# One attention stage: the prompt's differential heads beside twenty of the sample's differential units

## What is computed

```
def diff_core(q, k, v, qpos, kpos, bias_b, lam, lam_init, subln_g):
    logits = einsum('bqhcd,bkhcd->bhcqk', q, k) * (B_HEAD_DIM ** -0.5)
    logits = logits + bias_b[rel_bucket(qpos[:, None] - kpos[None, :])]
    p = softmax(where(kpos <= qpos, logits, -inf))
    w = p[:, :, 0] - lam * p[:, :, 1]
    o = einsum('bhqk,bkhe->bqhe', w, v)
    o = rmsnorm(o, subln_g) * (1.0 - lam_init)

def indexer_scores(qi, wi, ki):
    dots = einsum('bqhd,bkd->bqhk', qi, ki) * (IDX_DIM ** -0.5)
    return einsum('bqhk,bqh->bqk', relu(dots), wi * (IDX_HEADS ** -0.5))
```

## Time and profile before

| what | us |
|---|---|
| median of 3 runs (lowest to highest) | 2587.86 (2584.32 to 2591.13) |
| the profiled execution, its own time | 2581.11 |
| span of its trace | 2579.3 |
| differential stage, from its first logits | 417.0 to 594.5 |
| selective and sample stage, up to the next stage's first matmul | 594.5 to 1317.4 |

### The profile page before, as it was taken

How to read it: one execution, slowest core, us unless ns; L and a number is a source line. 1 busy time by engine, 2 the same in 40 slices (tenths; PEclk the granted TensorE clock), 3 DMA queues, 4 the chain that set the end, 5 groups by cost and what they waited for, 6 DMA issues and landing times. The chain is left out here.

```text
span 2579.3 us, 32477 instructions
## 1 busy us (share of the span) xinstructions
PE 2339.3 (91%) x12461; PEld 1574.9 (61%) x12461; DVE 1090.7 (42%) x2441; ACT 688.9 (27%) x1721; POOL 679.4 (26%) x722
## 2 busy tenths in 40 slices
PE   6999997885788888888889898989999999999999
PEld 4644444563455555555544445548888888888887
DVE  4479997881245533244323212253433343371001
ACT  2321112453555445544411014311111111110000
POOL 1020121112465455556601010013222121201110
PEclk9999997997999999998999999999999999999999
DMA  3211101004699789865640204111111111122221
GB/s 135 74 60 71 42 1 41 1 1 147 233 340 335 250 311 325 301 191 164 177 168 0 70 12 163 41 60 34 50 34 50 34 51 46 38 65 75 75 61 41
DMA packets 148605, 281.74 MB, mean 109 GB/s; under 512 B 14485, under 2 KB 83780, under 8 KB 148452
## 3 DMA queue, kind: packets, MB, share of 16 engines
q0 software_dynamic: 49408, 176.19, 20.1%
q1 hardware_dynamic: 80756, 90.50, 10.7%
q10 hardware_dynamic: 18288, 12.98, 1.7%
HBM read 261.68 MB, written 17.94 MB: 108 GB/s over the span
## 5 line engine op out<-in xcount | busy, mean ns | idle before, releaser
L607 PE MATMUL PS<-region 128*128 128x512 f32 (+5 forms) x864 | 330.6, 538 | 4.1 <-DMA region<-w_in 4.1
L2575 PE MATMUL PS<-region,ffn_w 128*128 128x264 f32 x1408 | 323.4, 388 | 1.6 <-PEq L2026 1.6
L2575 PEld LDWEIGHTS PS<-region,ffn_w 128*128 128x128 f32 x1408 | 269.4, 191 | 48.6 <-issue 2.0
L607 PEld LDWEIGHTS PS<-region 128*128 128x128 f32 (+1 forms) x864 | 154.3, 183 | 166.5 <-issue 140.6
L2575 PE MATMUL PS<-region,side 128*128 128x264 f32 x1056 | 243.3, 387 | 1.5 <-POOL side L2532 1.5
L1816 ACT COPY region<-PS 128x512 f32<-128x512 f32 x352 | 193.6, 594 | 183.4 <-PE PS L1695 96.5
L2575 PEld LDWEIGHTS PS<-region,side 128*128 128x128 f32 x1056 | 198.9, 190 | 35.0 <-POOL side L2532 1.6
L851 DVE TENSOR_SCALAR_CACHE_REDUCE mask<-score,cand 128x384 bf16<-128x384 f32 (+2 forms) x198 | 181.5, 942 | 3.2
L1559 POOL DMA_INDIRECT region<-cache_b_v,gather_b x128 | 122.6, 958 | 90.1 <-PE PS L1778 53.0
L2530 POOL TENSOR_TENSOR side<-ffn_w 128x512 f32<-128x512 f32 x22 | 29.2, 1326 | 391.7 <-DMA ffn_w<-w_gate 197.6
L1778 PE MATMUL PS<-region,sa_pt 128*32 128x512 f32 (+1 forms) x1024 | 86.4, 470 | 28.1 <-DMA region<-cache_b_v,gather_b 19.9
(11 more groups left out here) (429 smaller groups left out, 3977.3 us busy)
## 6 DMA issues: line engine op xcount, KB each, us to landing
ffn_w<-w_gate SPq DMA_DIRECT2D x11, 1024.0 KB, 5.4
ffn_w<-w_up SPq DMA_DIRECT2D x11, 1024.0 KB, 5.5
region<-w_in SPq DMA_DIRECT2D x4, 2048.0 KB, 7.9
ffn_w<-w_down ACTq DMA_DIRECT2D x7, 704.0 KB, 5.4
region<-x_prompt ACTq DMA_DIRECT2D x8, 512.0 KB, 7.3
region<-x_prompt SPq DMA_DIRECT2D x8, 512.0 KB, 10.6
mem_keys<-cache_mem_k SPq DMA_DIRECT2D x8, 512.0 KB, 4.6
mem_values<-cache_mem_v SPq DMA_DIRECT2D x8, 512.0 KB, 7.6
```

The source lines that it names most:

```text
L607: last = nc.tensor.matmul(M.PS[0:n, s % 3, 0:chunks[j].width], XT[:, c, t * P:t * P + n], w[j % 2][:, c, 0:chunks[j].width], start=(c == 0 ...
L2575: last = nc.tensor.matmul(M.PS[:, bank, 0:TW], left[:, c, :], right[:, c, :], start=begin and c == 0, stop=(c == KH - 1), skip_group_check ...
```

## The change

There is one attention stage now, in two halves, and 20 of the 32 B units run in its first half (`Walk.EARLY`).

- First half: the sample's B units 0 to 19 (and one chunk of new tokens) beside the prompt's differential heads. Their steps are L (logits, bias, maxima), E (exponentials, combination), T, V, and once a block N (norm: DVE, then POOL's power), R (scaling, DVE, in SBUF) and M (turning). The heads have one slot pair, one `prob`, one `pt` and one output bank: the combination overwrites `prob`, the transposes overwrite the logits' slot, and the logits of head n wait for the squares of head n-1 (`o_sq`). No count steps c are in this half. Key buffers are single here: `aside` and its two further buffers are used after unit 20 only, since they lie where `KTB` and the values of the prompt lie.
- Second half: the indexer, B units 20 to 31, A units, beside the selective pairs. Three c steps for each chunk instead of two.
- `beside` gets costs: L and E count 3.0 and other prompt steps 1.0, so that most sample steps stand behind L and behind E; an i step counts 4.0. First half: 145 sample and 152 prompt steps, of which 128 are L, E, T, V. Second half: 254 and 128.
- The relus of the indexer go from ACT (one instruction for a step) to DVE (two).
- POOL follows the same merged order; the last key step of unit 19 and its outputs release the first indexer gathers.
- The barrier between the two stages is gone. The clearing of semaphores stands ahead of the joint stage. `bias_a` lies in `KTB` now, so its load waits until the last differential logits (`s_ready`), and the first selective pair waits for all squares, all turned blocks and the end of the prompt's search (`freed`). Several small tiles moved to other places; their sizes aren't changed.

```diff
+    steps = []
+    for n, (i, h) in enumerate(heads):
+        begun = h == 0 and i > 0
+        steps += [("L", n)] + [("R", i - 1)] * begun + [("E", n)] + [("M", i - 1)] * begun + [("T", n), ("V", n)]
+        if h == B_H - 1:
+            steps.append(("N", i))
+    steps += [("R", NB - 1), ("M", NB - 1)]
...
+    prob = M.X[:, 0:2, :]
+    pt = M.X[:, 2, :].rearrange("p (k q) -> p k q", q=P)
+    mix = M.X[:, 3, :].rearrange("p (e n) -> p e n", e=2)
...
+    def sync(eng):
+        eng.dma_start(M.bias_b, head_bias(M, A_H, 12)).then_inc(b_loaded, 16)
+        rows = io["p_b_v"][0, 0].rearrange("(t p) h d -> p t (h d)", p=P)
+        for x, (a, b) in enumerate(((0, 2), (2, NB))):
+            eng.dma_start(M.VB[:, a:b, :], rows[:, a:b, :]).then_inc(v_loaded[x], 16)
+        eng.wait_ge(s_ready, 2 * N)
...
+    def pe(eng):
+        for what, n in steps:
+            if what == "L":
+                i, h = heads[n]
+                nk = (i + 1) * P
+                if n:
+                    eng.wait_ge(o_sq, n)
+                if turned_blocks(n):
+                    eng.wait_ge(m_read, turned_blocks(n))
+                for a, b in parts(0, nk):
...
+            elif what == "T":
+                eng.wait_ge(comb_done, n + 1)
+                for blocks in groups(n):
+                    for kb in blocks:
+                        last = nc.tensor.transpose(slot(0, kb * P, (kb + 1) * P), prob[:, 0, kb * P:(kb + 1) * P],
+                                                   K("ident"))
+                    last.then_inc(tr_done, 1)
+            elif what == "V":
+                i, h = heads[n]
+                if h == 0 and i in (0, 2):
+                    eng.wait_ge(v_loaded[i // 2], 16)
+                for x, blocks in enumerate(groups(n)):
+                    eng.wait_ge(pt_ready, groups_before(n) + x + 1)
+                    for kb in blocks:
+                        last = nc.tensor.matmul(M.PS[:, 2, 0:P], pt[:, kb, :], M.VB[:, kb, h * P:(h + 1) * P],
+                                                start=(kb == 0), stop=(kb == i))
+                last.then_inc(pv_done, 1)
...
+            elif what == "M":
+                eng.wait_ge(mix_done, n + 1)
+                if n < NB - 1:
+                    eng.wait_ge(s_used, 2 * (B_H * (n + 1) + 1))
+                for h in range(B_H):
+                    last = nc.tensor.transpose(M.PS[:, 3, h * P:(h + 1) * P], mix[:, n % 2, h * P:(h + 1) * P], K("ident"))
+                last.then_inc(mt_done, 1)
...
+    def act(eng):
+        for what, n in steps:
+            if what == "E":
+                nk = (heads[n][0] + 1) * P
+                for k in range(2):
+                    eng.wait_ge(max_done, 2 * n + k + 1)
+                    nc.scalar.activation(prob[:, k, 0:nk], slot(k, 0, nk), ACT.Exp, bias=negmax[:, k:k + 1],
+                                         accum_out=psum_[:, k:k + 1]).then_inc(s_used, 1)
+            elif what == "T":
+                for x, blocks in enumerate(groups(n)):
+                    a, m = blocks[0], len(blocks)
+                    eng.wait_ge(tr_done, groups_before(n) + x + 1)
+                    nc.scalar.copy(pt[:, a:a + m, :], slot(0, a * P, (a + m) * P).rearrange("p (k q) -> p k q", k=m)
+                                   ).then_inc(pt_ready, 1)
+            elif what == "V":
+                i, h = heads[n]
+                eng.wait_ge(pv_done, n + 1)
+                nc.scalar.copy(mix[:, i % 2, h * P:(h + 1) * P], M.PS[:, 2, 0:P])
+                nc.scalar.activation(osq[:], M.PS[:, 2, 0:P], ACT.Square, accum_out=oss[:, i % 2, h:h + 1]
+                                     ).then_inc(o_sq, 1)
...
+            elif what == "V":
+                M.top.rounds(link, share)
+            elif what == "N":
+                eng.wait_ge(o_sq, B_H * (n + 1))
+                nc.vector.scalar_tensor_tensor(oms[:, n % 2, :], oss[:, n % 2, :], 1.0 / (2 * HD), eps[:, n % 2, :],
+                                               ALU.mult, ALU.add).then_inc(o_ms, 1)
+            elif what == "R":
+                eng.wait_ge(o_rstd, n + 1)
+                for h in range(B_H):
+                    m = mix[:, n % 2, h * P:(h + 1) * P]
+                    last = nc.vector.scalar_tensor_tensor(m, m, ors[:, n % 2, h:h + 1], M.gain_sub[:], ALU.mult, ALU.mult)
+                last.then_inc(mix_done, 1)
+            elif n == NB - 1 and what == "M":
                 M.top.rounds(link, 1e6)
+                nc.vector.memset(M.sa_score[:, SEGW:SEGW + NS], NEG).then_inc(top_done, 1)
...
+        turn = [step[0] for step in walk.steps].index("i")
+        order = [1, 1] + beside(walk.steps[:turn], b_steps[2:], lambda step: 1.0, lambda step: 3.0 if step[0] in "LE" else 1.0)
+        order += beside(walk.steps[turn:], a_steps, lambda step: 4.0 if step[0] == "i" else 1.0,
+                        lambda step: 3.0 if step[0] in "LE" else 1.0)
...
-                pool_part(pool)
+                run(s_pool(pool), itertools.chain(b_pool(pool), iter(a_steps)))
...
+        self.steps = [("k", 0, j) for j in range(4)] + [("s", 0)]
+        for n in range(end + 1):
+            keys = [("k", n + 1, j) for j in range(1 if self.new(n + 1) else 4)] if n < end else []
+            if n == self.pause:
+                self.steps += [("p", n), ("o", n)]
+                for h in range(NCI):
+                    self.steps += [("i", h, g, a) for g in range(2) for a in range(2)] + [("I", h)]
+                self.steps += keys
+            else:
+                cut = iter(range(33)) if n == 0 else cut
+                late = n > self.pause
+                self.steps += keys[:3] + [("p", n)] + [("c", r) for r in itertools.islice(cut, late)]
+                self.steps += keys[3:] + [("o", n)] + [("c", r) for r in itertools.islice(cut, late)]
+            if n < end:
+                self.steps.append(("s", n + 1))
+                self.steps += [("c", r) for r in itertools.islice(cut, n > self.pause)]
+            if self.new(n):
+                self.steps.append(("f", n))
...
-        return u < self.first_a and u % 2 == 1
+        return self.EARLY < u < self.first_a and (u - self.EARLY) % 2 == 1
...
+        if u in (0, self.EARLY, self.EARLY + 1):
+            return None
+        if u < self.EARLY:
+            return u - 1
...
+        for step in steps:
+            if step[0] == "k" and not walk.new(step[1]):
+                n, j = step[1:]
+                u = walk.unit(n)
+                eng.wait_ge(t_full, fill["k", n, j, 1 if chunks[n][0] == "B" else 0] + 1)
+                if n == walk.pause:
+                    index(0, 0, j)
+                for v in range(len(walk.units)):
+                    if walk.keys_before(v) == u:
+                        keys(v, j)
...
-                relu(rel[:, g, :].rearrange("p (q a e) -> p e a q", a=RKI // 2, e=2)[:, :, 4 * a4:4 * a4 + 4, :],
-                     M.PS[:, L0:L1 + 1, :].rearrange("p e (a q) -> p e a q", a=4), n_i)
...
+        n_i = 0
         for step in steps:
-            if step[0] == "I" and step[1] == NCI - 1:
+            if step[0] == "i":
+                h, g, a4 = step[1:]
+                eng.wait_ge(i_done, n_i + 1)
+                for e in range(2):
+                    last = nc.vector.tensor_scalar(
+                        rel[:, g, :].rearrange("p (q a e) -> p e a q", a=RKI // 2, e=2)[:, e, 4 * a4:4 * a4 + 4, :],
+                        M.PS[:, L0 + e, :].rearrange("p (a q) -> p a q", a=4), HD ** -0.5 * IDX_H ** -0.5, 0.0,
+                        ALU.mult, ALU.max)
+                last.then_inc(relu_done, 1)
```

441 lines of the change are left out of this document (168 added, 273 removed).

## The result

The changed kernel takes 2597.29 us (median of six, 2589.13 to 2598.17) beside 2585.94 for the kernel before (six, 2582.23 to 2591.13). Ratio 1.0042, 95% interval 1.0026 to 1.0057: slower by some 11 us. The forecast was 2573, faster. The time lies inside the range of 2525 to 2615, on the side that had a chance of 0.25.

The account below looks back on a forecast made before the run. PE in its written order was taken as the bound. First half 385 plus second half 500 (56 + 189 + 255) gave 885 against 900 us, so the median 2587.9 less 15: 2573 us, range 2525 to 2615.

Parts of the forecast that it names:

- 385 + 500: The joint stage as first half plus second half: 885 us against 900 before, 15 us less.
- the rest is PE work at some share: Second half after the index part: 383 us of PE work, priced by busy shares of 88.5% and 83.5%.
- Index part 56: Start of second half: eight index steps 34, two score steps 8, four pairs of heads 14, together 56 us.
- The relus hidden: Indexer relus on DVE: 0.7 us per 512 columns, 1.4 a step, hidden beside the next key transposes.
- Twelve units 189: Second half's remaining B units: 167 us of PE work at an 88.5% share, 189 us.
- Last part 255: Sixteen A units and selective pairs: 216 us of PE work at 83.5%, less 4 for the clock, 255 us.
- First half 385: Differential heads beside 20 units: heads 371 us, start 8, block turns 6; PE busy 302 us, 78%.
- The walked chain: One differential head at the last block as a single dependent chain from logits to squares: 13.3 us.
- B: Rival: uncovered head chain; decides from a 12.1 us mean a head, at 13.1 33 us more, 2621; chance 0.18.
- C: Rival: second half takes what the first gives, stretch 906 or 896 us, 2584 to 2594 us; chance 0.17.
- A: Rival: laid-over regimes let PE reach 87% in all parts, 55 us less, 2533 us; chance 0.20.
- The search behind V: First half: the prompt's top-k search on DVE is covered; without cover its 25 counts would be 30 us.

Follow-up runs that it names:

- f1: Changed kernel with all step costs 1.0 in the second half only, first half unchanged: 2552.0 us, ratio 0.9863 to the kernel before.
- flat order: Step order of the changed kernel when all step costs are 1.0; with it in both halves 2551.03 us, ratio 0.9871.
- m_filled: Changed kernel, all step costs 1.0 in both halves, plus five idle transposes ahead of each differential head's transposes: 2545.69 us, ratio 0.9842.
- h_flat: Changed kernel with all step costs 1.0 in both halves, run on a slower chip: 2664.0 us, ratio 0.9794 to the kernel before.
- h_filled: Same slower chip as h_flat, its kernel plus five idle transposes ahead of each differential head's transposes: 2654.0 us, ratio 0.9739.
- h_flat_no_search: h_flat with the rest of the prompt's top-k search left out: 2659.3 us, ratio 0.9771.
- f3: Changed kernel; in the second half index steps cost 1 while L and E keep 3: 2588.4 us, ratio 1.0010.
- f2: Changed kernel; in the second half index steps keep cost 4 while L and E cost 1: 2579.9 us, ratio 0.9986.
- e1_flat: Changed kernel with all step costs 1.0 in both halves, nothing else changed: 2551.03 us, ratio 0.9871 to the kernel before.

## Why the prediction was wrong

The forecast was a gain of 15 us in the sum of "385 + 500"; the stretch became 5.2 us longer, 905.5 instead of 900.3.

**Where the sign came from.** The step that failed is "the rest is PE work at some share": the second half was priced as busy time over a share taken from the stretches of before (88.5% and 83.5%), and the new costs entered only as a number of pairs moved. That the costs also set the distance between E, T and V wasn't priced. The runs show that the costs of the second half are worth 45 us, 2597 to 2552 (f1): they turn a gain of 1.4% (32 us beside the kernel before of the same chip) into a loss of 0.4% (11 us). Without them the forecast's direction would have been right: 2552 is the lower end of its own range (2552 to 2588). The prediction walked one differential head through the order, but never one selective pair.

The miss of the total was made smaller by luck. The terms 385, 56, 189 and 255 describe the flat order, as their shares come from stretches of it; f1 measures 404, 54, 185 and 223, 866 in all. So the order was left out at 40 us in this stretch, and without it the sum was 19 too high: 32 in the last part, less 19 in the first half.

**"Index part 56."** Measured 71. The prediction's work was right (45 and 5, 50 in all; measured 50.9), so the miss is in how long PE stands: 6 us were left for it, and 20 measured. By steps, with the waits ahead of them, the eight index steps took 39.6 us (34 predicted), the two score steps 16.0 (8), the four pairs 15.5 (14). So more than half of the miss is the score steps (L1656), and not the order's doing: they take 16.8 in f1, and already in the kernel before one alone took 8.3 behind a stand of 2:

```profile
633.50 8.32 PE L1651 MATMUL PS<-side,sa_w_sel 128*32 128x512 f32 x16 [2.04 <-ACT side L1820]
```

With flat costs the part takes 54, since index steps fall to 34.2 and three of the four pairs move out of it. "The relus hidden" was right, their size wasn't: DVE took 1.02 us for 512 columns (sixteen, 15.1 us) and not 0.7, so as much as ACT's 1.89 a step, and above the bound of 0.95. Put back on ACT, nothing changed.

**"Twelve units 189"** at 88.5%: measured 196.3 at 84%; f1 184.6 at 89%. The share was right for an order with two steps on each place. **"Last part 255"**: 236. Its work was overpriced, 216 for a measured 194, and the share was right (82%). The prediction took the 190 us of 1086 to 1318 for the sixteen A units. But in the kernel before their first transposes (L1688) come at 1111.8 only; ahead of them 18.7 us of work, the last B unit's, the group's new tokens' and part of a pair's, lie in that stretch. The A units with ten pairs were:

```profile
1111.70:1317.40 205.70, 170.65 (x1613) 114.33 (x1612) 84.40 (x188) 89.89 (x208) 118.57 (x122) 0.94 0.54 154
```

From there, five more pairs added 23 us, 4.6 each and not 5.5. The 19 us that the last part came out shorter hid the other two.

**"First half 385."** Measured 402, and 398 to 405 in six further runs on these chips. The sum of the waits was right: 385 less 302 of work leaves 83 us, and PE stood for 79. The walked chain came out too (13.3, alone 13.8), in part by luck, as said above. The term that was mis-sized is PE's work, 323 instead of 302. The 302 are the heads' 142 of before, at a clock of 0.91, and 20 x 8.0 for the units, whose 8.0 were read where the clock was 0.98. In the first half, whose clock is 0.91 (0.88 on the slower chip), a unit is dearer: from 16 to 20 units PE's busy time there grew by 36 us, 9.0 a unit, and 142 + 20 x 9.0 is 322. At the better clock of m_filled (0.94) the useful work took about 303. That the filling gives back some 10 of the 17 us speaks for the clock as a cause; but h_flat and h_filled, the only pair on one chip, have intervals that just meet, so this is likely and not shown. By heads: 10.0 us at block 0 and 10.5 at block 1 (8.5 and 9.1 predicted), 15.0 and 17.0 at the last two (14.4 and 15.7).

**The rivals.** B's condition was just reached. It named a mean of 12.1 us, (371 + 16)/32, without the 14 us for the start and the turns; measured is (402 - 14)/32, also 12.1. It isn't why the kernel is slower: with the same first half the flat kernels are 32 us faster than before. C's total, 906, is the measured 905.5, by other terms (first half 385, index 66, twelve units 192, last part 263), so by luck. For A, the Trainium skill ("Perfetto Trace Analysis", Optimization Strategy) says that interleaving regimes may gain; the flat kernel agrees, with PE at 83% (717 of 865 us) and not at 87%.

**Costed at nothing.** The search behind V: right (h_flat_no_search). The load of `bias_a`: right, no wait for it is in the lists. The gathers beside the combinations: right within 5 us, as the first half's 160 gathers took 0.96 (keys) and 0.99 us (values) in the mean against 0.94. The 23 of them that overlap a combination (L1181) took 1.08 in the mean, up to 1.73, the others 0.95. The prediction's "0.55 otherwise" was read too widely, though: most of the other powers ran into the start of a combination, which has two SBUF inputs as well, and still took 0.55; only the one that ran wholly beside such an operation took 1.58. The clearing of semaphores: wrong, since it now lies ahead of the first logits, which come 3.7 us later (the stand for PEq there is 5.1 us and was 2.0).

## What to carry to other kernels

When two streams are merged by costs, the costs are not only a balance of work: they set how many foreign steps stand between an instruction and the one that waits for its result. Walk one unit of each stream through the merged order before taking a share of busy time as its price, and look for places with no or one step behind work that another engine must copy. Cut the stretches that give the prices at the events that the names mean, such as the first transposes of the A units, and not near them: 19 us of this prediction's last part were another part's. A busy time holds the clock of the stretch that it was read in. Where PE has to stand for a few microseconds anyway, idle transposes into a free bank may gain a little through the clock; here it was 6 to 10 us of 2550, at the edge of what the runs can tell.

## What the runs showed of the hardware

Short stands of PE were followed by work at either of the two rates, and neither their length nor the instructions decide it. In the changed kernel's index part transposes took 0.24 us each instead of 0.14 behind a stand of 1.62, where slow work had begun already, and 0.14 behind stands of 1.64 and 1.86. The same sixteen score matmuls stand behind the same wait in f1 and in f3, and took 5.37 and 7.04 us:

```profile
870.07 5.37 PE L1655 MATMUL PS<-side,gain_ak 128*32 128x512 f32 x16 [2.02 <-DVE side L1914]
```

```profile
869.74 7.04 PE L1655 MATMUL PS<-side,gain_ak 128*32 128x512 f32 x16 [2.02 <-DVE side L1914]
```

In f2's index part, with 7.0 us of waits before V, the work was some 13 us longer than in f1 (17 less the 4 of the added pairs).

Two chips take 2721 and 2723 us for the kernel before, three others 2583 to 2587. In the flat kernel the extra is all in this stage: the first logits come at 420.7 there and 420.1 here, what lies behind the stage takes 1263 and 1264 us of the span, and this stage 979 and 865. What differs there is seen in the wait lists: ACT, DVE and POOL have waits whose releaser the profile doesn't find ("remote"). Between 415 and 1440 us they come to 115 us for ACT and 77 for DVE in h_flat, and there are none in before, after, e1_flat, f1 or m_filled. Two of h_flat's lines, 857 to 1399 us:

```profile
ACT QTA L1301 <- remote: 45.6, 10, 7.2
...
DVE sa_cmax L1937 <- remote: 29.2, 10, 4.2
```

One such wait ends for both engines at nearly the same time, at 1004.45 (DVE, 4.19 us) and 1004.54 (ACT, 6.21 us). PE waits for their results, and its busy time in the stage is longer too, 760 us against 717, at a lower clock (0.88, 0.91 and 0.93 in the three parts, against 0.90, 0.97 and 0.98). What those engines wait for is open. The flat kernel gains 2.1% on such a chip instead of 1.3%.
